# RWKV-7 in a hybrid decoder step: the last of the six merges of a triangular inverse multiplies only the 64x64 corners that are not zero

## The reference

```
def step(S, inp):
    r_t, d_t, k_t, v_t, kk_t, a_t = inp
    sa = jnp.einsum('bhvk,bhk->bhv', S, kk_t)
    S = S * d_t[:, :, None, :] - sa[..., None] * (kk_t * a_t)[:, :, None, :] + v_t[..., None] * k_t[:, :, None, :]
    return S, jnp.einsum('bhvk,bhk->bhv', S, r_t)
```

## Time and profile before

| | |
|---|---|
| median of 3 runs | 4526.83 us (4526.81 to 4541.08) |
| the profiled execution | 4531.75 us; its span 4530.2 us |
| PE, PEld, DVE busy | 84%, 77%, 75% of the span |
| RWKV stage, 640 to 1430 us | 790 us: PE busy 656.23, DVE 435.93, ACT 193.36 us; granted clock of PE 0.84 |
| experts, 2508 to 4478 us | 1970 us: PE busy 1963.92 us, granted clock 1.00 |

### The profile page before, as it was taken

One profiled execution on the slowest core, in us unless ns is written; L12 is line 12 of the kernel. 1 busy time (PEld: TensorE's weight loads), 2 busy tenths in 40 slices (PEclk: granted clock), 3 DMA queues, 4 the chain that ended last, 5 costly groups with the idle time before them and its releaser, 6 DMA issues. The chain is left out here.

```text
span 4530.2 us, 66470 instructions
## 1 busy us (share of the span) xinstructions
PE 3783.7 (84%) x22546; PEld 3474.4 (77%) x22546; DVE 3411.6 (75%) x7027; ACT 1025.8 (23%) x1637; POOL 1225.8 (27%) x1054
## 2 busy tenths in 40 slices
PE   7996757888985877651554999999999999999997
PEld 6996645777774844430554899999999999999997
DVE  5322545576553169998998799999999999999998
ACT  3212232232221101110222322222222222222221
POOL 1120000000000000000000455555655655555553
PEclk8998667898886989875999999999999999999998
DMA  3674130000002000000233888888888888888885
GB/s 92 85 81 93 59 95 5 18 28 11 1 8 98 24 22 32 21 36 2 111 148 162 307 290 300 294 288 300 294 288 301 294 288 300 293 289 300 291 291 197
DMA packets 292097, 729.40 MB, mean 161 GB/s; under 512 B 27529, under 2 KB 138841, under 8 KB 290449
## 3 DMA queue, kind: packets, MB, share of 16 engines
q0 software_dynamic: 120560, 431.42, 30.7%
q1 hardware_dynamic: 171424, 296.57, 19.4%
HBM read 650.20 MB, written 77.70 MB: 161 GB/s over the span
## 5 line engine op out<-in xcount | busy, mean ns | idle before, releaser
L2416 POOL DMA_INDIRECT experts_u_row<-in_up_rows,experts_u_at x384 | 542.7, 1413 | 645.5 <-DVE experts_dot L2602 530.1
L107 PE MATMUL experts_down_ps<-experts_act_hi,experts_down_hi 128*128 128x352 f32 x2048 | 677.4, 331 | 8.8 <-DVE experts_down_lo L2578 6.8
L107 PE MATMUL experts_up_ps<-experts_u_hi,experts_up_hi 128*128 128x352 f32 x2048 | 662.1, 323 | 26.1 <-DVE experts_u_lo L2578 24.9
L108 PE MATMUL experts_down_ps<-experts_act_lo,experts_down_hi 128*128 128x352 f32 x2048 | 661.3, 323 | 0.0
L108 PE MATMUL experts_up_ps<-experts_u_lo,experts_up_hi 128*128 128x352 f32 x2048 | 660.8, 323 | 0.0
L109 PE MATMUL experts_up_ps<-experts_u_hi,experts_up_lo 128*128 128x352 f32 x2048 | 660.6, 323 | 0.0
L109 PE MATMUL experts_down_ps<-experts_act_hi,experts_down_lo 128*128 128x352 f32 x2048 | 660.5, 323 | 0.0
L2423 POOL DMA_INDIRECT experts_v_row<-in_down,experts_v_at x384 | 511.3, 1331 | 241.4 <-issue 104.0
L2602 DVE CUSTOM_DVE_ANT_0 experts_u_row<-experts_u_row,stream_u_rows_of 128x1024 f32<-128x1024 f32 x384 | 467.0, 1217 | 67.2 <-DMA experts_u_row<-in_up_rows,experts_u_at 67.2
L2615 DVE SCALAR_TENSOR_TENSOR stream_h_rows_of<-experts_v_row,experts_weight,stream_h_rows_of 128x1024 f32<-128x1024 f32 x384 | 498.0, 1298 | 13.0 <-DVE experts_weight L2607 6.6
L2621 DVE TENSOR_TENSOR stream_h<-stream_h,experts_down_ps 128x704 f32<-128x704 f32 x512 | 451.1, 881 | 73.2 <-PE experts_down_ps L109 72.9
(11 more groups left out here) (364 smaller groups left out, 6561.5 us busy)
## 6 DMA issues: line engine op xcount, KB each, us to landing
experts_up<-in_up SPq DMA_DIRECT2D x128, 512.0 KB, 6.6
experts_down<-in_down SPq DMA_DIRECT2D x128, 512.0 KB, 7.0
gates<-spread_spread SPq DMA_DIRECT2D x11, 4096.0 KB, 11.3
experts_gates<-gates SPq DMA_DIRECT2D x64, 704.0 KB, 7.1
cols<-inp_done POOLq DMA_DIRECT2D x27, 576.0 KB, 10.1
inp_w_in<-in_w_in SPq DMA_DIRECT2D x27, 512.0 KB, 6.7
pick_w_query<-in_w_query SPq DMA_DIRECT2D x16, 512.0 KB, 4.0
experts_u_row<-in_up_rows,experts_u_at POOLq DMA_INDIRECT x384, 6.4
```

The source lines that it names most:

```text
L107: pe.matmul(out, w_hi, x_hi, start=start, stop=False)
L108: pe.matmul(out, w_hi, x_lo, start=False, stop=False)
L2416: pool.indirect_dma_start(u_row[b][:], None, up_rows_d, bass.IndirectOffsetOnAxis(ap=u_at[slot][:, b, a:a + 1], axis=0)).then_inc(u_row_lo ...
```

## The change

For l = 6, x, `neg_x`, z and the add are cut to the 64x64 corners. `FIRST` is rows or columns 0 to 63, `SECOND` 64 to 127. The instructions are the same in number, order, semaphores and buffers; 20 merges (16 with m = 4, 4 with m = 2) have them in smaller shapes. The x matmuls go from 128 contracted rows, 128 stationary and 128 moving columns to 64, 64 and 64; the z matmuls from 128, 128 and 64 to 64, 64 and 64. The ACT copy goes from 128 partitions by m*128 elements to 64 by m*64. The DVE add goes from 128 partitions to 64 with the same m*64 elements in each. Merges 1 to 5 are as before.

```diff
+FIRST, SECOND = slice(0, P // 2), slice(P // 2, P)
@@ -1141,7 +1143,8 @@
-                    act.activation(neg_x[:, 0:group.m, :], x_quads(group.m), ACT.Copy, scale=-1.0).then_inc(x_ready, 1)
+                    rows, cols = (slice(0, P), slice(0, P)) if l < LEVELS - 1 else (SECOND, FIRST)
+                    act.activation(neg_x[rows, 0:group.m, cols], x_quads(group.m)[rows, :, cols], ACT.Copy, scale=-1.0).then_inc(x_ready, 1)
@@ -1361,8 +1364,11 @@
-                    t = half_cols(inv_t[:, 0:m, :], l, 1)
-                    dve.tensor_tensor(t, t, pieces(1), ALU.add).then_inc(merged, 1)
+                        t = half_cols(inv_t[:, 0:m, :], l, 1)
+                        dve.tensor_tensor(t, t, pieces(1), ALU.add).then_inc(merged, 1)
+                    else:
+                        t = inv_t[FIRST, 0:m, SECOND]
+                        dve.tensor_tensor(t, t, z_half(1, m)[FIRST, :, :], ALU.add).then_inc(merged, 1)
@@ -1563,7 +1569,10 @@
-                        mm = pe.matmul(x[:, i, :], join[:, i, :], inv[:, i, :], start=True, stop=True)
+                        if l < LEVELS - 1:
+                            mm = pe.matmul(x[:, i, :], join[:, i, :], inv[:, i, :], start=True, stop=True)
+                        else:
+                            mm = pe.matmul(x[SECOND, i, FIRST], join[FIRST, i, SECOND], inv[FIRST, i, FIRST], start=True, stop=True)
...
-                        mm = pe.matmul(z_half(1, m)[:, i, :], neg_x[:, i, :], half_cols(inv_t[:, i:i + 1, :], l, 1)[:, 0], start=True, stop=True)
+                        if l < LEVELS - 1:
+                            mm = pe.matmul(z_half(1, m)[:, i, :], neg_x[:, i, :], half_cols(inv_t[:, i:i + 1, :], l, 1)[:, 0], start=True, stop=True)
+                        else:
+                            mm = pe.matmul(z_half(1, m)[FIRST, i, :], neg_x[SECOND, i, FIRST], inv_t[SECOND, i, SECOND], start=True, stop=True)
```

## The result

The changed kernel takes 4546.82 us (median of 18 runs, 4537.77 to 4562.95); the kernel before takes 4528.07 us on the same chip (18 runs, 4523.30 to 4542.87). The ratio is 1.0040, with an interval of 1.0029 to 1.0051: 18.7 us slower. The forecast was 4520.5 us, faster instead of slower, and the measured time lies 15 us above the upper end of the range, 4532. What happened is rival 2, the clock, but for the most part not where the prediction had put it.

The account below looks back on a forecast made before the run. In the RWKV stage no engine is full; the chain x, copy, z, add sets the pace. Savings of 1.9 + 1.1 + 1.7 + 0.4 + 1.2 = 6.3 us from 4526.8 gave 4520.5 us, range 4511 to 4532.

Parts of the forecast that it names:

- rival 2: PE falls to 1.2 GHz in last merges, 1.9 us each; four cancel the gain, all eleven give +15 us; chance 0.10.
- The cost of a small pass: Last-merge x and z: a 64-column load steps at about 0.06 us instead of 0.111, eight passes saving 0.36 us.
- Rival 1: Small passes in the last merges get no cheaper while new switches cost time: +1 us, 4528; chance 0.12.
- The switch of shape: PE changing matmul shape beside new x or z: 0.20 us, or 0.15 if the load behind has 64 columns.
- kind A: Last merges of groups 3, 8, 13, DVE waiting 0.86 or 0.87 us for z: 0.63 us won each, 1.9 in all.
- kind D: Last merges of groups 18 and 19, DVE waiting 0.22 us for z: all of it won, 0.4 us in all.
- kind B: Last merges of groups 9 and 14, DVE waiting 0.54 us for z: all of it won, 1.1 us in all.
- Kind C: Last merges of groups 5, 10, 15, ahead of a new pair, waiting 0.78 us: 0.58 won each, 1.7 us in all.
- kind E: Last merge of the last group, at clock 0.50, DVE waiting 4.93 us for z: 1.2 us won.
- the ceilings: DVE's waits for z in last merges, 11.4 us in all; once DVE waits no more, faster z gives nothing.
- Nothing should take it back: Behind the last-merge add, DVE's list, next loads and later stages move with it, so the 6.3 us stay won.
- the eleven: Last merges, of 20, whose add waits for z, 11.4 us together; in the other nine DVE is late, nothing won.

Follow-up runs that it names:

- e2: Changed kernel with all 128 contracted rows kept in last x and z (128x64x64 each): ratio 0.9990 to the kernel before.
- f1: Kernel before plus unread 128x128x128 matmuls ahead of x in every merge, two each and three in the last: ratio 0.9947.
- f4: Kernel before plus unread matmuls with 8 moving columns (128x128x8) ahead of x in every merge: ratio 1.0040 to the kernel before.
- e9: Changed kernel with z full again and last x at 128x128x64, copy and add small: ratio 1.0045 to the kernel before.
- e11: Changed kernel with z full again and last x at 64x128x64, copy and add small: ratio 1.0049 to the kernel before.
- e4: Changed kernel with z given its full shape back, last x still 64x64x64: ratio 1.0036 to the kernel before.
- e7: Changed kernel plus five unread 128x128x8 matmuls per last merge, ahead of x and behind z: ratio 1.0021 to the kernel before.
- f2: Changed kernel plus unread 128x128x128 matmuls ahead of x in every merge and two behind the last z: ratio 0.9970 to the kernel before.
- f3: Kernel with last x and z at 128x64x64, plus unread 128x128x128 matmuls in every merge and two behind the last z: ratio 0.9955 to the kernel before.
- e5: Kernel before with only the last x cut to 64 moving columns (128x128x64): ratio 1.0057 to the kernel before.
- e10: Changed kernel with z full again and last x at 128x64x64, copy and add small: ratio 0.9978 to the kernel before.
- e12: The changed kernel run again as control on another chip: ratio 1.0034 to the kernel before.

## Why the prediction was wrong

- **The cost of a small pass: right.** Eight loads in 0.54 us, x 0.65 and z 0.68, where 0.06 us a step was forecast for 0.111. Rival 1 is out. It rested in part on the rule of the Trainium skill (page "TensorE: Matmul & The Clock Gate", Part 3) that a load overlaps with running matmuls only in another row group, and the trace doesn't agree with it here: all passes of the new x go to the same rows of the array, and eight loads that take 0.54 us by themselves take 0.65 together with their matmuls.
- **The switch of shape: too dear.** The prediction read the earlier trace rows as if L1481's first pass came 0.04 us behind the end of L1522, but the row has that matmul start at 983.40, 0.07 ahead of it. New z starts 0.06 us before the end of L1487 (1179.24 + 0.91) where the old one started 0.16 before: a switch of 0.10 us and not 0.15.
- **The sum at full clock: right as far as it can be seen.** Last x to next x went from 4.43 to 3.71 us in the 8th and the 13th group (0.72; kind A said 0.63) and from 3.79 to 3.47 in the 18th (0.32; kind D 0.22), all at the full clock. From 5.38 and 5.37 to 4.74 in the 9th and 14th (0.64; kind B 0.54) holds some clock as well, since before PE was at 1.2 GHz for a part of it. Kind C never ran at the full clock in the changed kernel, and kind E only there. In e2, whose loads are as short and whose clock held, kind C shows 4.52 to 3.71 (0.81, where 0.58 was forecast), and the last merges of the first 19 groups are 5.3 us shorter in all; the forecast has 5.1 for them. The unchanged add (0.41 us) was right; the ceilings were passed by 0.1 us in kinds B and D.
- **"Nothing should take it back": wrong.** The unchanged merges took back 27 us. The sum has no term for the clock of merges that the change doesn't touch; it was put at nothing.
- **Rival 2: its price near, its place too narrow.** It let the clock fall only in the last merges themselves, 1.9 us each, and called four of them decisive. Five of the eleven (3rd, 5th, 10th, 15th and 19th group) do run at 1.2 GHz for a part where before they didn't, and are 0.4 to 1.8 us longer than before, 1.4 us on average against the forecast. With what the others gain, the last merges cancel. The loss is in merges 1 to 5 and what is woven into them, the 10.7 us up to the twelfth group's last x among it.
- **Rival 2's dismissal, the step that failed.** "Kind A's bursts fill 3.87 of 4.00 us and less than 0.8 of that goes away" counted busy time, and only that of the last merge, and gave the rival 0.10. f1 against f4 shows that nearly equal busy time of PE raises the clock or leaves it as it was, by its moving columns (0.94 and 0.89 in the stage, 0.88 without a fill), and e9 to e11 with e4 that what the last x feeds per us sorts the ratios. The change cut what x feeds to a quarter and its load time only to 0.56 (0.54 us for 0.97).
- What the prediction named as its refutation, a clock of the stage under 0.82, is what came: 0.84 in the earlier trace rows, 0.78 now (0.79 if the window is kept at 640 to 1430 us).

The Trainium skill (page "TensorE: Matmul & The Clock Gate", Part 1) ties the clock to how busy PE has been. These runs agree in part: matmuls put into PE's waits raised the clock of the merges from 0.88 to 0.94. They differ in what a busy us is worth, since the same number of matmuls with 8 moving columns left it at 0.89.

**Open:** what in the moving columns and rows acts on the clock, since no run takes the reading of the operand apart from the multiplying or the writing to PSUM; whether it matters that x stands right behind the idle 0.94 us; how much of e7's gain is real; why f2 gains less than f1 and f3; and which instructions made up 5 us between the merges and the experts. The split between the last merges and the others is read from one execution of each version, and isn't the same in all: in e5 the last merges have more of the loss than the others (8.5 us against 3.4).

## What to carry to other kernels

In a stage that a chain holds and where the granted clock moves between its levels, ask of an edit on PE not only what time it saves but also whether its bursts still feed as many rows times moving columns in a us; the loss may appear in work beside it. Where only a corner of a matmul is needed, cut the stationary and the moving columns together, which nearly halves the burst, and keep the contracted rows: 0.998 to 0.999 here (the 0.999 is not told from 1). Cutting the rows, or the moving columns under full stationary ones, gave 1.003 to 1.006. Full-height matmuls with 128 moving columns that nobody reads, put ahead of PE's waits, were worth 0.5% without any change to the work; with 8 moving columns they cost 0.4% (their target here is x's own bank, ahead of x and behind z).

## What the runs showed of the hardware

- Two streams of matmuls with equal loads and nearly equal busy time (0.61 and 0.51 us for four) gave granted clocks of 0.94 and 0.89 over 673 and 701 us of merges, where the kernel without them has 0.88; only the moving columns, 128 and 8, differed (f1, f4).
- In bursts with 64 or 128 moving columns an f32 pass costs what its stationary columns cost: eight loads 0.97 us with 128, 0.54 with 64, whether 128 or 64 rows (e10, the change). Rows save nothing: 7 loads of 64x128 take 0.85 us in e11, the same step as 8 in 0.97. The Trainium skill says the same of a load (page "TensorE: Matmul & The Clock Gate", section "LDWEIGHTS (loading the stationary operand)"), and the trace agrees.
- In e4, where only x with its copy and the add is smaller, 20 bursts of x (144 of the 4120 passes, about 14 us of PE's time) went with a stage of 715.6 us instead of 688.4 and a clock of 0.82 instead of 0.88, in one profiled execution each; over all runs the ratio is 1.0036.
- Executions of the unchanged kernel on one chip differ by up to 21 us, and their times go with their granted clocks: 2.8 us for each 0.001 (23 executions beside e9 to e12).
